# Mixer 3's first projection on raw tokens, and the last down chunk block by block

## The reference

```python
h = h + swiglu(rms_norm_2(h, norm_ffn_g[l]), ffn_w_gate[e], ffn_w_up[e], ffn_w_down[e])
...
hn = rms_norm_2(h, norm_mix_g[l])          # h / rms(h) * gamma, per token
q, f, i, g = jnp.split(hn @ w_in, 4, axis=-1)
log_f = jnp.logaddexp(jnp.log(lb), jnp.log1p(-lb) + jax.nn.log_sigmoid(f))
k = (1.0 - lb) * jax.nn.sigmoid(-f)
qh = jax.nn.silu(heads(q)) * (HGRN_DK ** -0.5)
o = gated_chunkwise(qh, k, heads(i), log_f)
```

## Time and profile before

| | us |
|---|---|
| median of 3 runs | 2111.53 |
| lowest, highest | 2111.31, 2113.92 |
| the profiled execution | 2112.26 |
| its span | 2110.4 |
| TensorE (PE) busy in it | 1962.5 (93%) |
| VectorE (DVE) busy | 630.2 (30%) |
| ScalarE (ACT) busy | 459.3 (22%) |
| GpSimd (POOL) busy | 92.5 (4%) |

### The profile page before, as it was taken

The page is one execution under the profiler, slowest core; times in us unless marked ns, Lnnn a source line. Parts: engine busy times, 40 slices in busy tenths (PEclk is TensorE's granted clock), DMA queues, the critical chain, the costliest instruction groups (busy, mean ns, idle before and its releaser), DMA issues.

```text
span 2110.4 us, 38658 instructions
## 1 busy us (share of the span) xinstructions
PE 1962.5 (93%) x17015; PEld 1241.6 (59%) x17015; DVE 630.2 (30%) x1142; ACT 459.3 (22%) x641; POOL 92.5 (4%) x38
## 2 busy tenths in 40 slices
PE   9989987888777999999999999999999998999997
PEld 8888543433344999999999873433333433333433
DVE  5762311111111773544476640010011010011011
ACT  4621111100112443344366320010000010000011
POOL 4520000000000100000100000000000000000000
PEclk9999888878898899999999999999999999999999
DMA  8253699999999531455634339999999999999995
GB/s 323 89 199 120 246 422 424 425 425 424 422 425 387 183 120 61 146 191 183 227 133 159 121 142 340 378 420 419 418 419 418 416 418 419 418 418 418 408 407 245
DMA packets 134767, 653.11 MB, mean 309 GB/s; under 512 B 9824, under 2 KB 32480, under 8 KB 89440
## 3 DMA queue, kind: packets, MB, share of 16 engines
q1 hardware_dynamic: 134624, 650.95, 77.4%
HBM read 649.87 MB, written 1.05 MB: 308 GB/s over the span
## 4 chain that ended last, share of the span: by engine, by line
PE 72%; DMA 18%; DVE 5%; ACT 2%; SPq 1%; issue 1%; DVEq 0%; ACTq 0%
PE psum L2031 17%; DMA ring<-in_w_gate 12%; PE psum L2096 7%; PE psum L2037 6%; PE psum L551 6%; PE psum L552 6%; PE psum L553 6%; PE psum L1667 4%; PE psum L724 3%; DMA arena<-in_moe_w_down 3%; PE psum L2101 3%; DMA ring<-in_w_down 2%; PE psum L2404 1%; PE psum L585 1%; SPq L450 1%
## 5 line engine op out<-in xcount | busy, mean ns | idle before, releaser
L2031 PE MATMUL psum<-ring,arena 128*32 128x384 f32 (+1 forms) x3584 | 368.2, 541 | 1.2 <-issue 0.6
L553 PE MATMUL psum<-ring_r 128*128 128x256 f32 x944 | 266.4, 282 | 0.0
L2031 PEld LDWEIGHTS psum<-ring,arena 128*32 128x32 f32 x3584 | 117.5, 110 | 213.8 <-issue 208.8
L2096 PE MATMUL psum<-ring,arena 128*32 128x512 f32 x1600 | 197.7, 593 | 12.9 <-ACT arena L2193 6.9
L1667 PE MATMUL psum<-ring,arena 128*32 128x512 f32 x896 | 153.6, 757 | 52.2 <-DMA ring<-in_w_gate 49.5
L553 PEld LDWEIGHTS psum<-ring_r 128*128 128x128 f32 x944 | 179.7, 190 | 0.0
L551 PE MATMUL psum<-ring_r 128*128 128x256 f32 x608 | 176.0, 290 | 0.4 <-DVE ring_r L615 0.3
L552 PE MATMUL psum<-ring_r 128*128 128x256 f32 x608 | 172.0, 283 | 0.0
L2278 DVE TENSOR_TENSOR arena<-arena,psum 128x512 f32<-128x512 f32 (+1 forms) x42 | 23.8, 617 | 384.0 <-issue 348.0
L1667 PEld LDWEIGHTS psum<-ring,arena 128*32 128x32 f32 x896 | 38.9, 135 | 160.2 <-issue 158.3
L2037 PE MATMUL psum<-ring,arena 128*32 128x512 f32 (+1 forms) x1120 | 131.6, 539 | 0.0
(11 more groups left out here) (424 smaller groups left out, 2855.4 us busy)
## 6 DMA issues: line engine op xcount, KB each, us to landing
ring<-in_w_gate SPq DMA_DIRECT2D x64, 1024.0 KB, 21.5
ring<-in_moe_w_gate SPq DMA_DIRECT2D x64, 1024.0 KB, 19.2
ring<-in_moe_w_down SPq DMA_DIRECT2D x64, 1024.0 KB, 18.9
ring<-in_w_up SPq DMA_DIRECT2D x48, 1024.0 KB, 24.7
ring<-in_w_down SPq DMA_DIRECT2D x24, 2048.0 KB, 25.7
ring<-in_moe_w_up SPq DMA_DIRECT2D x48, 1024.0 KB, 19.5
ring<-in_moe_w_gate SPq DMA_DIRECT2D x64, 768.0 KB, 18.2
ring<-in_moe_w_up SPq DMA_DIRECT2D x48, 768.0 KB, 17.0
```

What stands on the lines that cost most here:

```text
L553: return nc.tensor.matmul(out, al, bh, start=False, stop=stop, **kw)
L2031: mm = nc.tensor.matmul(bank(b0 + j)[n * MORE:(n + 1) * MORE, 0:Q], z_Xg[:, x:x + MORE], w[:, (2 * h + j) * Q:(2 * h + j + 1) * Q], start= ...
L2096: mm = nc.tensor.matmul(bank(6)[tile * MORE:(tile + 1) * MORE, :], z_hidT[:, x:x + MORE], rows_of(half, 0, 512), start=first, stop=last)
```

## The change

1. `down` of the last chunk goes output block by output block and signals after each pair (`out_0` to `out_3`). VectorE adds each pair when it is signalled and multiplies it by gamma right behind.
2. The first projection, hf0, takes tokens times gamma that are not divided by the norm. ScalarE rounds each quarter of `hT` (`raw_hi`), VectorE subtracts (`raw_lo`). They and the squares have tiles of their own. The sums of squares are taken by TensorE between the two halves of hf0. The warming matmuls are gone.
3. When the norm factor is there, `hT` is multiplied by it and the normalised tokens are made for all other projections. Each half of hf0's result is multiplied by the factor on VectorE (`scaled`), out of PSUM, before Exp.
4. hq0's high weights of its first two quarters are made before the norm factor; their low parts are made on GpSimd instead of VectorE. hq0's first quarter waits for the normalised tokens quarter by quarter.

```diff
+        def raw_hi(act, st, raw, r):
+            act.wait_ge(*V[st].at(f"gain{r}"))
+            nc.scalar.activation(quarter(raw[0], r), quarter(hT, r), ACT.Copy).then_inc(*S[st].step())
+            S[st].name(f"raw_hi{r}")
+
+        def raw_lo(dve, st, raw, r):
+            dve.wait_ge(*S[st].at(f"raw_hi{r}"))
+            nc.vector.tensor_tensor(quarter(raw[1], r), quarter(hT, r), quarter(raw[0], r).bitcast(F32),
+                                    ALU.subtract).then_inc(*V[st].step())
+            V[st].name(f"raw_lo{r}")
...
         def project(pe, st, part, name, free, quarters=range(4), first=False):
...
+                    if first and q == 0 and k % 2 == 0:
+                        pe.wait_ge(*S[st].at(f"tok_hi{k // 2}"))
+                        pe.wait_ge(*V[st].at(f"tok_lo{k // 2}"))
...
             def down(n, c):
                 _, lo, hi, _, name = ffn_unit(n)
                 pe.wait_ge(*v.at(f"hid_lo{c}"))
+                if c == FFC - 1:
+                    for d in range(KC):
+                        x = slice(d * P, (d + 1) * P)
+                        for f in range(2):
+                            y = slice(f * T, (f + 1) * T)
+                            mm = three(bank(4 + d // 2)[:, (d % 2) * T:(d % 2 + 1) * T], (hi[:, f, x], lo[:, f, x]),
+                                       (f_hid_hi[c % 2][:, y], f_hid_lo[c % 2][:, y]), False, f == 1,
+                                       skip_group_check=True)
+                        if d % 2:
+                            mm.then_inc(*e.step())
+                            e.name(f"out_{d // 2}")
...
-            dve.wait_ge(*e.at(f"ffn_d{FFC - 1}_1"))
             for b in range(4):
+                dve.wait_ge(*e.at(f"out_{b}"))
                 x = xT[:, 2 * b:2 * b + 2, :]
                 nc.vector.tensor_tensor(x, x, bank(4 + b).rearrange("p (b t) -> p b t", t=T), ALU.add)\
                     .then_inc(*v.step())
                 v.name(f"x_d_{b}")
+                with_gain(dve, "hgrn", param("mix2_g", 8, 8), b, v.last())
             v.name("x")
-            for r in range(4):
-                with_gain(dve, "hgrn", param("mix2_g", 8, 8), r, v.at(f"x_d_{r}"))
...
+        h_raw = [carve_r(2400 + KC * T * n, KC * T).rearrange("p (k t) -> p k t", t=T) for n in range(2)]
+        h_sq = carve(2400 + 2 * KC * T, KC * T)
...
-            keep_warm(3, 8)
-            pe.wait_ge(*V["ffn"].at("x"))
-            for r in range(4):
-                norm_tensor(pe, st, r)
-            keep_warm(6, 10)
-            project_first(pe, st, "two", "hf0")
+            def sums():
+                for r in range(4):
+                    norm_tensor(pe, st, r, h_sq)
+
+            project_first(pe, st, "two", "hf0", sums, h_raw, RAW_NAMES)
...
+            proj("hq0", first=True)
+            proj("hi0")
...  (ScalarE)
-            norm_scalar(act, st, residual("ffn", "d"))
-            tokens_hi(act, st)
-
+            for r in range(4):
+                raw_hi(act, st, h_raw, r)
+                nc.scalar.activation(h_sq[:, r * 512:(r + 1) * 512].rearrange("p (k t) -> p k t", t=T), quarter(xT, r),
+                                     ACT.Square).then_inc(*s.step())
+                s.name(f"n_sq{r}")
             act.wait_ge(*v.at("lbdiff"))
             nc.scalar.activation(c_small[:, 40:56], c_small[:, 40:56], ACT.Exp).then_inc(*s.step())
             s.name("lbexp")
+            round_next(act, st, "two", PROJ3, "hf0", 0)
+            act.wait_ge(*e.at("n_sum"))
+            nc.scalar.activation(RSTD, bank(7)[:, 0:T], ACT.Ln, bias=eps_col, scale=1.0 / D).then_inc(*s.step())
+            act.wait_ge(*s.last())
+            nc.scalar.activation(RSTD, RSTD, ACT.Exp, scale=-0.5).then_inc(*s.step())
+            s.name("n_rstd")
+            tokens_hi(act, st)
             act.wait_ge(*v.at("bounds"))
...
             for part in range(2):
-                keep(0, "f", halves(HG[0].k), func=ACT.Exp, scale=-1.0, parts=(part,))
+                if part:
+                    round_next(act, st, "two", PROJ3, "hf0", 1)
+                act.wait_ge(*v.at(f"hf0_scaled{part}"))
+                f = HG[0].k[:, part * 512:(part + 1) * 512]
+                nc.scalar.activation(f, f, ACT.Exp, scale=-1.0).then_inc(*s.step())
+                s.name(f"hf0_{part}")
                 sigmoid(0, part)
...  (GpSimd)
             weights_lo_of(nc.gpsimd, G, "hgrn", "two", "hf0")
+            weights_lo_of(nc.gpsimd, G, "hgrn", "two", "hq0", (0, 1))
...  (VectorE)
+            for r in range(4):
+                raw_lo(dve, st, h_raw, r)
             do(nc.vector.tensor_tensor(m, lb[:, 0:8], lb[:, 8:16], ALU.max))
...
-            normed(dve, st)
-            tokens_lo(dve, st)
             dve.wait_ge(*s.at("lbexp"))
...
+            def scaled(part):
+                dve.wait_ge(*e.at(f"hf0_{part}"))
+                nc.vector.tensor_tensor(HG[0].k[:, part * 512:(part + 1) * 512].rearrange("p (b t) -> p b t", t=T),
+                                        bank(2 * (B3 % 2) + part).rearrange("p (b t) -> p b t", t=T),
+                                        RSTD.unsqueeze(1).to_broadcast([P, 2, T]), ALU.mult).then_inc(*v.step())
+                v.name(f"hf0_scaled{part}")
+
+            normed(dve, st)
+            scaled(0)
+            tokens_lo(dve, st)
+            scaled(1)
...
             for part in range(2):
                 forget_start(0, part)
-                lo_on_vector(st, "hq0", (2 * part, 2 * part + 1))
+                if part:
+                    lo_on_vector(st, "hq0", (2, 3))
```

More of the change, by code:

```diff
@@ L576, in tokens_lo, with first_product @@
                 V[st].name(f"tok_lo{r}")
-        def first_product(pe, st, out, w, columns, done):
+        TOK_NAMES, RAW_NAMES = ("tok_hi", "tok_lo"), ("raw_hi", "raw_lo")
+        def raw_hi(act, st, raw, r):
[7 more added lines that the diff above has]
+            V[st].name(f"raw_lo{r}")
+        def first_product(pe, st, out, w, columns, done, tokens=tok, names=TOK_NAMES):
             for n, c in enumerate(columns):
@@ L582, in first_product @@
                     if n == 0 and k % 2 == 0:
-                        pe.wait_ge(*S[st].at(f"tok_hi{k // 2}"))
+                        pe.wait_ge(*S[st].at(f"{names[0]}{k // 2}"))
                     for m in range(2):
-                        nc.tensor.matmul(out(n), w[m][:, k, c], tok[0][:, k, :], start=(n == 0 and k == 0 and m == 0),
+                        nc.tensor.matmul(out(n), w[m][:, k, c], tokens[0][:, k, :], start=(n == 0 and k == 0 and m == 0),
                                          stop=False, skip_group_check=True)
@@ L626, in lo_ready @@
         def lo_ready(st, name, q):
+            if name == "hq0" and q < 2:
+                return G[st].at(f"{name}_lo{q}")
             return (V if (name == "q" and q < 2 or st == "mix1" and (name == "z" or name == "a_b" and q >= 2)
@@ L630, in lo_ready, with project_first @@
                 .at(f"{name}_lo{q}")
-        def project_first(pe, st, part, name, between=lambda: None):
+        def project_first(pe, st, part, name, between=lambda: None, tokens=tok, names=TOK_NAMES):
             lo = ring_r[slot_of(part, name)][:, :].rearrange("p (k n) -> p k n", n=512)
@@ L645, in project_first @@
                 first_product(pe, st, lambda n: bank(b0 + half)[:, n * T:(n + 1) * T], (w_hi, lo),
-                              [slice(q * P, (q + 1) * P) for q in (2 * half, 2 * half + 1)], done)
+                              [slice(q * P, (q + 1) * P) for q in (2 * half, 2 * half + 1)], done, tokens, names)
                 E[st].name(f"{name}_{half}")
@@ L649, in project_first, with project @@
                     between()
-        def project(pe, st, part, name, free, quarters=range(4)):
+        def project(pe, st, part, name, free, quarters=range(4), first=False):
             lo = ring_r[slot_of(part, name)][:, :].rearrange("p (k n) -> p k n", n=512)
@@ L3166, in hgrn_tensor, with proj @@
             e, s, v = E[st], S[st], V[st]
-            keep_warm(3, 8)
-            pe.wait_ge(*V["ffn"].at("x"))
-            for r in range(4):
-                norm_tensor(pe, st, r)
-            keep_warm(6, 10)
-            project_first(pe, st, "two", "hf0")
-            def proj(name, quarters=range(4)):
+            def sums():
+                for r in range(4):
+                    norm_tensor(pe, st, r, h_sq)
+            project_first(pe, st, "two", "hf0", sums, h_raw, RAW_NAMES)
+            def proj(name, quarters=range(4), **kw):
                 (project_rows if name[1] == "i" else project)(
-                    pe, st, "two", name, free_by(st, PROJ3, name, lambda n, half: [s.at(f"{n}_{half}")]), quarters)
-            for what in "qi":
-                proj(f"h{what}0")
+                    pe, st, "two", name, free_by(st, PROJ3, name, lambda n, half: [s.at(f"{n}_{half}")]), quarters,
+                    **kw)
+            proj("hq0", first=True)
+            proj("hi0")
             pe.wait_ge(*s.at("hq0_1"))
```

13 lines of the change are left out of this document (7 added, 6 removed).

## The result

The changed kernel took 2119.24 us (median of 9 runs, 2115.83 to 2121.81), the kernel before 2111.53 in the same session: ratio 1.003 [1.0022, 1.0039], that is 6.3 us slower (4.6 to 8.2); the two medians themselves lie 7.7 apart, the two means 6.7. The forecast was 2114.8 (+3.3) in a range of 2109.6 to 2117.6, so the median lies outside it. Run again in two other sessions the changed kernel stood at 1.0035 [1.0022, 1.0048] and 1.0043 [1.003, 1.0055]. The profiled execution took 2116.72, among the lowest of the nine, its span 2114.5.

What follows compares the result with a forecast made beforehand. TensorE, with 72% of the chain, was taken to bound the kernel. Terms 1.1 + 1.3 + 0.85 = +3.3 us took the profiled 2112.26 to 2115.5, and the median 0.7 below gave 2114.8, range 2109.6 to 2117.6.

Steps and rivals of the forecast that it cites:

- Part 4: TensorE's clock may fall behind waits at hf0's start and in hq0: 1.3 and 0.85 us, each bounded by 0 and 1.7.
- Part 1: Last down chunk by block: GpSimd's subtractions hold VectorE's gain products, the last done at 1054.65 instead of 1051.4 unheld.
- rival A: At the last down chunk GpSimd does not hold gain products: 2110.9 or 2109.2 us; chance 0.17.
- Part 2: hf0 on raw tokens: three TensorE waits, first half done 1059.8, sums of squares 1063.3, second half 1069.1 against 1070.86 before.
- the first fall: TensorE's clock falling in the waits at hf0's start, delaying the sums of squares: 1.3 us, bounds 0 and 1.7.
- Part 3: hq0's third-quarter low weights come late, seen at 1077.75; TensorE waits 2.9 us and resumes 1.1 later than before.
- the first clock term: The 1.3 us taken for TensorE's slow clock in the waits at hf0's start.
- The chain's term: TensorE resuming in hq0 later than before because normalising starts later: +1.1 us, -2.3 and +1.8 at the bounds.
- The second: TensorE's clock falling behind the 2.9 us wait in hq0: 0.85 us, half of the bound 1.7.
- rival B: Gain products held, clock low for two stretches in the first gap and falling in hq0: +5.8 us, 2117.3; chance 0.12.

Runs made afterwards that it cites:

- warm2: Changed kernel plus twelve matmuls that nobody reads in TensorE's wait in hq0; 1.0016 of the kernel before.
- warm12: Changed kernel plus unread matmuls in hq0's wait and sixteen more in the three waits at hf0's start; 1.0014 of the kernel before.
- part2: Changed kernel with down products, adds and gain products in the old order; 1.0026 of the kernel before.
- pool_later: Changed kernel with GpSimd making hf0's last two low-weight quarters only after the fourth gain product; 2118.73 us, 1.0024 of the kernel before.
- clear: Changed kernel with GpSimd's last two hf0 quarters after the low raw tokens, hq0's first two low quarters on VectorE; 1.0015 of the kernel before.
- free: Changed kernel; VectorE makes hf0's last two and all hq0 low quarters, 128x8 differences precede adds, hq0's last two quarters split earlier; 2108.02 us, 0.9977 of the kernel before.
- again: The changed kernel, unaltered, run and traced a second time; 1.0035 of the kernel before.
- again_third: The changed kernel, unaltered, run for a third trace; 1.0043 of the kernel before.
- clear_warm: The kernel clear plus twelve unread matmuls in TensorE's wait of 3.1 us in hq0; 1.0004 of the kernel before.
- part1: Kernel before plus only down products by block, each gain product behind its add, and squares in their own tile; 1.0016 of the kernel before.

## Why the prediction was wrong

**Direction and mechanism.** Slower was forecast and came; the way there was as described, but the size was not. The price of the clock in Part 4 failed, and the sum had no term for what lies outside the span.

**Part 1 held.** Gain 3 was forecast done at 1054.65; it was at 1053.57 + 1.15 = 1054.72. The rule of the Trainium skill, page "SBUF — State Buffer", section "Who interferes with whom", was the reason to expect a tensor_tensor to be held as the scalar_tensor_tensor of the earlier trace rows was; the trace agrees, with 1.35, 2.18 and 2.14 beside 0.69, and rival A falls. Each hold ended with GpSimd's running instruction. GpSimd's four took 10.34 instead of 9.43, so VectorE's gain products delay GpSimd's as well; the prediction had let two of the four slip by 0.4 each.

**Part 2 held, but for what the clock took.** First half forecast done at 1059.8 and then the sums; with 1.3 for the first fall that is 1061.1; they began at 1060.87 on the scale of before. The three waits, counted from when the next product could have been issued, were 1.06, 2.19 and 0.3 where 1.1, 2.3 and 0.9 had been forecast; the third was shorter in part because the four products before it already ran at the low clock (0.21 each). The fall itself cost 0.9 (warm2 against warm12), less than the 1.3, in this trace; in the two others it lasted twice as long and the sums began 1.5 later still. Wrong in Part 2 is that the warming products taken out "are worth nothing by themselves": with the same waits and such products in them the clock stays whole (warm12).

**Part 3 held within some 0.4.** Low weights forecast ready at 1077.75, with the first clock term 1079.05; measured 1077.47 + 1.15 = 1078.62. The wait was forecast at 2.9 and was 2.8. The chain's term was +1.1; with the clock kept it measured +1.47 (warm12).

**Part 4 is the step that failed:** "The second I take at half, 0.85, as rows stand on both sides", with 1.7 as its bound. From the third quarter's first product to the scores it took 17.3 before (1076.6 to 1093.90) and 20.19 after (1077.50 to 1097.69): 2.9. Two things were mis-sized. The chance: in three traces of three the clock fell in hq0, and also behind the like waits of part2 (2.8), pool_later and clear (3.1). And the bound: 1.7 was read from one stretch at 1.2 GHz, but the clock was low from 1077 to 1083.6, about twice as long, while TensorE had no wait in it from 1077.50 on. In the two other traces the long stretch stood behind the first gap and the short one in hq0: the seam's clock cost in all was 3.5, 3.8 and 3.8 (scores less warm12's 56.49), against 2.15 taken and 3.4 as the most. Those two traces are rival B as written, two stretches in the first gap and a fall in hq0: the seam costs 5.3 there against B's 5.8. B had been given 0.12.

The trace of before could have told both. It has twelve waits of TensorE of 2 to 4 us. The clock fell at nine (those that end at 18.38, 93.47, 374.50, 404.18, 433.84, 463.51, 493.18, 582.19 and 1223.59) and stayed at three (315.16, 522.86, 611.86); the earlier trace rows show two of the nine and one of the three. And twelve times it was low for 6.8 us with TensorE busy throughout, each time soon after a wait of 1.4 to 1.5, as here, where the products after the wait begin at 300.67:
```profile
302.90:306.30 3.40, 3.40 (x12) 2.15 (x14) 1.36 (x3) 0.00 (x0) 0.00 (x0) 0.50 1.01 419
306.30:309.70 3.40, 3.40 (x20) 0.79 (x16) 0.46 (x1) 0.00 (x0) 0.00 (x0) 0.50 1.01 422
```

**Sum.** 1.5 for the chain and 3.5 for the clock are the 4.95 of the seam; 3.3 had been forecast, 1.1 and 2.15. These 1.7 alone would have moved the forecast to 2116.5, still inside the range. So the mis-sized clock alone does not explain the miss. The traced execution of after took 4.46 more than before's: 4.95 in the seam, 0.3 behind it, 0.36 outside the span, for which the sum had no term since it took 1.9 for both, and 1.15 less ahead of the seam. The sum then took the median as 0.7 below the traced execution; that holds for before, but the changed kernel's median is 2.5 above its traced one. That is 3.2 of the 7.7 between the medians; the time outside the span makes 0.7 on the mean of all runs, 0.36 of it already in the traced one, and the rest lies in executions that were not traced and stays open. The range ended at 2117.6 since B was its edge. A stretch of 6.8 us behind each gap, which no trace shows together, would by these traces cost 1.5 + 2.3 + 2.9 = 6.7 (an estimate: warm12's rest, 23.5 less 21.17, and the 2.9 above), so the range should have reached beyond B.

## What to carry to other kernels

When work is pulled forward on one engine, follow every queue that its forerunners stand in: here TensorE began early, and lost it 25 us later to a chain that had moved with the norm factor; moving one step forward in ScalarE's queue and one in VectorE's was worth 4.4 us, nearly the whole loss. Moving work of GpSimd next to other VectorE operations with two SBUF operands changes who is held (pool_later, clear); in free, with that work on VectorE and the small operations ahead of the adds, only the first gain product was held. In this kernel a TensorE wait of 2 to 3 us is to be priced as itself plus up to 2.9 of slow clock, and a dozen idle matmuls in it gave 2.6 back. Before a price is read from one row, count all rows of its kind in the trace: nine of twelve is not a toss.

## What the runs showed of the hardware

- A held operation waits until GpSimd's running instruction ends, whatever its own size: 128x8 operations of 0.16 to 0.17, issued within 0.1 of such an instruction's start, took 2.27 to 2.39 (clear, pool_later), a TENSOR_SCALAR with one tensor operand among them (2.31). GpSimd's own instructions were slowed by the 128x512 ones (2.82 and 2.85 instead of 2.4 in after), not by the 128x8 ones (2.40 and 2.35 in clear).
- After a wait of 2.8 us the slow stretch lasted about 3.4 us in three traces (again, again_third, part2) and about 6.8 in one (after), with TensorE busy from the wait's end on; behind the first gap with short bursts in it (about 3 us of waiting) once 3.4 and twice 6.8 in the three traces of the change.
- Twelve matmuls that nobody reads in the wait of 2.8 kept the clock at 1.00 behind it (warm2, warm12, and clear_warm for one of 3.1), and 4, 9 and 3 in the pieces of the first gap did so there (warm12).
- The time outside the span is 1.82 to 1.84 us on the mean of before's runs in each session and in part1, and 2.1 to 2.6 on the mean in all kernels with the raw tokens, free among them. What makes it is not shown.
